# Heads stage of a two-layer encoder trunk: transposes one product group later, first maxima in the last tiles, key tables in ten parts, rotary squares from the latents

## What is computed

```
p = h @ w_in_a                       # h = rmsnorm(x); q_lat 384, kv_lat 256, k_pe 32, ...
q = rmsnorm((rmsnorm(q_lat) @ w_uq).reshape(S, 12, 96)); rope on the last 32 of each head
kv = (rmsnorm(kv_lat) @ w_ukv).reshape(S, 12, 64 + 64)    # k_nope, v
k = rmsnorm(concat(k_nope, k_pe of all heads))            # its mean takes in sum(k_pe ** 2)
k = k * gain, rope on the last 32
o = softmax(q @ k.T * 96 ** -0.5) @ v
```

## Time and profile before

| | |
|---|---|
| median of 3 runs | 3332.96 us (3332.16 to 3334.99) |
| the profiled execution, its span | 3333.53 us, 3331.5 us |
| busy: PE, DVE, ACT, POOL | 96%, 60%, 52%, 42% of the span |
| heads on PE, first product to last transposes | 224.74 to 478.82 us |
| attention, first instruction | 487.49 us |
| DMA share from 262 to 454 us | 0.96 |

### The profile page before, as it was taken

How to read it: one execution, slowest core, us unless ns; L and a number is a source line. 1 busy time by engine, 2 the same in 40 slices (tenths; PEclk the granted TensorE clock), 3 DMA queues, 4 the chain that set the end, 5 groups by cost and what they waited for, 6 DMA issues and landing times. The chain is left out here.

```text
span 3331.5 us, 46492 instructions
## 1 busy us (share of the span) xinstructions
PE 3198.4 (96%) x17548; PEld 2753.4 (83%) x17548; DVE 1991.6 (60%) x2820; ACT 1717.4 (52%) x2514; POOL 1407.4 (42%) x916
## 2 busy tenths in 40 slices
PE   7979979999999999999979999999999979999999
PEld 7978867777777777777769999887888869999787
DVE  5637878888888888888853334445333344333432
ACT  4536646777777777777754455113223234544200
POOL 2227867999999999999920000000111000000000
PEclk9989989999999999999989999999999989999999
DMA  8958983333213333321043223987232243223565
GB/s 305 341 209 294 357 290 80 78 73 77 64 42 66 70 66 68 70 50 42 19 153 101 101 92 108 269 247 227 107 111 98 85 179 126 89 96 105 159 198 152
DMA packets 380334, 454.87 MB, mean 137 GB/s; under 512 B 51800, under 2 KB 317400, under 8 KB 367824
## 3 DMA queue, kind: packets, MB, share of 16 engines
q1 hardware_dynamic: 380112, 451.91, 44.1%
HBM read 262.07 MB, written 189.64 MB: 136 GB/s over the span
## 5 line engine op out<-in xcount | busy, mean ns | idle before, releaser
L1330 POOL TENSOR_TENSOR at_acc<-at_acc,at_ph 128x1024 f32<-128x1024 f32 x288 | 691.2, 2400 | 63.5 <-ACT at_ph L1254 48.1
L1375 DVE TENSOR_TENSOR at_pl<-at_sc,at_ph 128x1024 fp32r<-128x1024 f32 x408 | 498.9, 1223 | 127.0 <-ACT at_sc L1255 122.7
L1254 ACT ACTIVATE at_ph<-at_sc 128x1024 fp32r<-128x1024 f32 x408 | 418.9, 1027 | 289.3 <-PE at_sc L1174 280.9
L1363 DVE TENSOR_REDUCE at_mx<-at_mxp 128x1 f32<-128x512 f32 x816 | 521.5, 680 | 34.4 <-PE at_mxp L1185 34.2
L1255 ACT ACTIVATE at_sc<-at_sc 128x1024 f32<-128x1024 f32 x408 | 415.7, 1019 | 0.0
L1199 PE MATMUL at_o_hi<-at_ph,at_v 128*128 128x512 f32 x816 | 322.9, 396 | 0.6 <-issue 0.6
L1201 PE MATMUL at_o_lo<-at_pl,at_v 128*97 128x512 f32 x816 | 322.2, 395 | 0.0
L1758 POOL TENSOR_TENSOR gm_rstd<-gm_mean,all_mhalf 128x4 f32<-128x4 f32 x40 | 40.3, 1007 | 616.3 <-DVE gm_mean L1898 616.3
L171 PE MATMUL ou_acc<-ou_o_hi,ou_og 128*128 128x512 f32 x640 | 251.7, 393 | 13.4 <-DVE ou_og L2133 12.1
L172 PE MATMUL ou_acc<-ou_o_lo,ou_og 128*128 128x512 f32 x640 | 250.7, 392 | 0.0
L173 PE MATMUL ou_acc<-ou_o_hi,ou_og 128*128 128x512 f32 x640 | 250.5, 391 | 0.0
(11 more groups left out here) (294 smaller groups left out, 8701.7 us busy)
## 6 DMA issues: line engine op xcount, KB each, us to landing
hT<-lat_n_h SPq DMA_DIRECT2D x28, 1024.0 KB, 7.3
h_first<-hT SPq DMA_DIRECT2D x24, 1024.0 KB, 7.8
h_second<-hT SPq DMA_DIRECT2D x24, 1024.0 KB, 7.1
qT<-hd_stq SPq DMA_DIRECT2D x60, 384.0 KB, 6.4
kT<-hd_stk SPq DMA_DIRECT2D x60, 384.0 KB, 6.0
ka_q<-qT SPq DMA_DIRECT2D x120, 192.0 KB, 3.0
sgT<-gm_sg SPq DMA_DIRECT2D x80, 256.0 KB, 2.2
h_first<-omix SPq DMA_DIRECT2D x40, 512.0 KB, 6.2
```

What stands on the lines that cost most here:

```text
L1254: act.activation(ph[:, g], sc[g % 2][:], ACT.Exp, scale=SCALE).then_inc(p_hi, 1)
L1330: pool.tensor_tensor(acc[:, c.slot, :], f32(ph[:, (g - 1) % 4]).rearrange("p b n -> p (b n)") if t == 1 else acc[:, c.slot, :], now, ALU.a ...
L1363: dve.tensor_reduce(mx[:, c.slot, n:n + 1], mxp[n % 2][:], AX.X, ALU.max).then_inc(mx_in, 1)
L1375: dve.tensor_tensor(pl[:, g], sc[g % 2][:], f32(ph[:, g]), ALU.subtract).then_inc(p_lo, 1)
```

## The change

1. On PE each group of transposes stands one product group later: the first two groups of keys after the second and third query group, the third after the first key-value group, the first two groups of queries after the second and third key-value group, the third after the first query group of the next tile. DVE's and ACT's order stays, except at tile 0, where the low values go ahead of the key mean.
2. The first chunk's 16 maxima are made in `heads`, in the banks `pq`, beside the transposes from tile 19's second key-value group on (`BESIDE`), in the order of the key blocks; keys of tiles 12 to 15 are loaded in step 19, and the row of the negated maxima is the last thing that SP issues in the stage. Waiting for the stores, and loading the keys of tiles 16 to 19, go to the start of attention; there chunk 0's first scores stand ahead of the six maxima of chunk 1.
3. The key tables are made two tiles at a time, in ten parts of six instructions: part 0 before the first query root, part p between the query rotation and the key root of tile 2p-2.
4. The mean of the rotary squares is taken by ACT in `latents`, one squaring of 32 columns with a sum per tile, and completed by one DVE instruction.

```diff
+def wait_stored(self, sp):
+    for u in range(2):
+        sp.wait_ge(self.v_out[u], 16 * TILES // 2)
+    for c in range(3):
+        sp.wait_ge(self.q_st[c], 16 * TILES)
+        sp.wait_ge(self.k_st[c], 16 * TILES)
+def row(self, sp, n, slot, quad):
+    sp.wait_ge(self.neg_in, n + 1)
+    for b in range(4):
+        sp.dma_start(f32(self.q[QK:QK + 1, quad, 0, b * P:(b + 1) * P]),
+                     f32(self.neg[:, slot, b:b + 1]), allow_slow_non_contiguous=True
+                     ).then_inc(self.row_in[slot], 16)
...
+    after(act, kpe_in, i)
+    act.activation(junk[:, QL + KVL:], a[:, 1, KVL:KW], ACT.Square, scale=float(QK) ** -0.5,
+                   accum_out=ahead.kpms[:, i:i + 1])
     act.copy(kpe_all[:, i, :], a[:, 1, KVL:KW]).then_inc(kpe_in, 1)
...
+    MAXIMA = sorted(range(16), key=lambda n: n % 4)
+    BESIDE = {(TILES - 1, "q", 0): 2, (TILES - 1, "q", 1): 2, (TILES - 1, "q", 2): 2, (TILES, "k", 0): 2,
+              (TILES, "k", 1): 2, (TILES, "k", 2): 2, (TILES, "q", 0): 1, (TILES, "q", 1): 1, (TILES, "q", 2): 2}
...
-        if t.n in (8, 12, 16):
-            sp.wait_ge(k_st[0], 16 * (t.n - 4))
-            keys.load_first(sp, kT, t.n - 8, t.n - 4)
+        if t.n in (8, 12, 16, 19):
+            last = (t.n + 1) // 4 * 4 - 4
+            sp.wait_ge(k_st[0], 16 * last)
+            keys.load_first(sp, kT, last - 4, last)
     run_tiles(DRAIN, step)
-    for u in range(2):
-        sp.wait_ge(v_out[u], 16 * TILES // 2)
-    for c in range(G):
-        sp.wait_ge(q_st[c], 16 * TILES)
-        sp.wait_ge(k_st[c], 16 * TILES)
-    keys.load_first(sp, kT, 12, TILES)
+    keys.row(sp, 0, 0, 0)
...
-    def queries(t, k_behind):
+    def maximum(n, of, c):
+        for at, piece in maxima_beside(n, of, c):
+            if at == 0:
+                pe.wait_ge(q_out, TILES)
+                pe.wait_ge(q_sq, TILES)
+                pe.wait_ge(keys.q_load[0], 32)
+            pe.wait_ge(keys.kh_load[0], 16 * (piece % 4 + 1))
+            after(pe, keys.mx_in, at - 2)
+            pe.matmul(pq[:, at % G, :], keys.q[0:QK, 0, 0, piece // 4 * P:(piece // 4 + 1) * P],
+                      keys.k0[0:QK, 0, piece % 4 * BLK:(piece % 4 + 1) * BLK], start=True, stop=True
+                      ).then_inc(keys.mx_mm, 1)
+    def queries(t, q_behind, k_behind):
         if t.within(TILES):
             pe.wait_ge(lat_in[t.slot], t.half * 16 + 16)
             after(pe, q_out, t.n)
...
                 if c == G - 1:
                     m.then_inc(q_mm, 1)
-            if k_behind.within(TILES):
-                turn_k(k_behind, c)
-    def keys_values(t, q_behind):
+            if c == 0 and q_behind.within(TILES):
+                turn_q(q_behind, G - 1)
+            if c > 0 and k_behind.within(TILES):
+                turn_k(k_behind, c - 1)
+            maximum(*((t.n - 1, "q", G - 1) if c == 0 else (t.n, "k", c - 1)))
+    def keys_values(t, k_behind, q_behind):
         if t.within(TILES):
             after(pe, k_out, t.n)
             after(pe, v_lo, t.n)
...
                 if c == G - 1:
                     m.then_inc(kv_mm, 1)
-            if q_behind.within(TILES):
-                turn_q(q_behind, c)
+            if c == 0 and k_behind.within(TILES):
+                turn_k(k_behind, G - 1)
+            if c > 0 and q_behind.within(TILES):
+                turn_q(q_behind, c - 1)
+            maximum(*((t.n, "k", G - 1) if c == 0 else (t.n, "q", c - 1)))
     def step(j, u):
-        queries(Tile(j, u), Tile(j, u, -2))
-        keys_values(Tile(j, u), Tile(j, u, -1))
+        queries(Tile(j, u), Tile(j, u, -2), Tile(j, u, -2))
+        keys_values(Tile(j, u), Tile(j, u, -2), Tile(j, u, -1))
...
-    def key_tables():
...
+    def key_tables(part):
+        ts, base = slice(part * PART, (part + 1) * PART), TABLES + part * PART_TABLES
+        cos, sin, rope, pe_rows = cosq[:, ts], sinq[:, ts], krope[:, ts], kpe_all[:, ts]
+        gains_of = lambda n: graw[:, n:n + 1, 0:RP].broadcast_to([P, PART, RP])
+        pool.wait_ge(made, base)
+        pool.tensor_tensor(cos, cos, gains_of(2), ALU.mult).then_inc(made, 1)
+        pool.tensor_tensor(sin, sin, gains_of(3), ALU.mult).then_inc(made, 1)
+        pool.wait_ge(made, base + 2)
+        pool.tensor_tensor(rope, pe_rows, cos, ALU.mult).then_inc(made, 1)
+        pool.wait_ge(made, base + 3)
+        pool.tensor_tensor(cos[:, :, 0:H], pe_rows[:, :, H:RP], sin[:, :, 0:H],
                            ALU.mult).then_inc(made, 1)
-        pool.tensor_tensor(cosq[:, :, H:RP], kpe_all[:, :, 0:H], sinq[:, :, H:RP],
+        pool.tensor_tensor(cos[:, :, H:RP], pe_rows[:, :, 0:H], sin[:, :, H:RP],
                            ALU.mult).then_inc(made, 1)
-        pool.wait_ge(made, 7)
-        pool.tensor_tensor(krope[:], krope[:], cosq[:], ALU.add).then_inc(made, 1)
-        pool.tensor_tensor(sinq[:], kpe_all[:], kpe_all[:], ALU.mult).then_inc(made, 1)
+        pool.wait_ge(made, base + 5)
+        pool.tensor_tensor(rope, rope, cos, ALU.add).then_inc(made, 1)
...
+        pool.wait_ge(made, TABLES + (t.n // PART + 1) * PART_TABLES)
...
         t = Tile(j, u)
+        if t.n == 0:
+            key_tables(0)
         query_root(t)
         query_rope(t)
-        if t.n == 0:
-            key_tables()
+        if t.n % 2 == 0 and t.n // 2 + 1 < PARTS:
+            key_tables(t.n // 2 + 1)
         key_root(t)
         key_rope(t)
     run_tiles(0, step)
+    pool.wait_ge(k_rope, TILES)
+    pool.memset(f32(keys.k0[QK:QK + 1, 0, :]), 1.0).then_inc(keys.ones_in, 1)
...
+    dve.tensor_scalar(kpms[:], kpms[:], EPS, 1.0, ALU.add, ALU.mult).then_inc(squares, 1)
+    dve.wait_ge(squares, 1)
...
+    def maxima(n, of, c):
+        for at, piece in maxima_beside(n, of, c):
+            dve.wait_ge(keys.mx_mm, at + 1)
+            dve.tensor_reduce(keys.mx[:, 0, piece:piece + 1], pq[:, at % G, :], AX.X, ALU.max
+                              ).then_inc(keys.mx_in, 1)
...
-    def key_squares():
-        dve.wait_ge(made, K_TABLES)
...
         if t1.within(TILES):
-            if t1.known and t1.n == 0:
-                key_squares()
+            if t1.n == 0:
+                value_lo(t1)
             key_mean(t1)
         if t2.within(TILES):
             low_k(t2, 0)
-        if t1.within(TILES):
+        maxima(t.n, "k", 0)
+        if t1.within(TILES) and t1.n > 0:
             value_lo(t1)
         if t2.within(TILES):
             low_k(t2, 1)
+            maxima(t.n, "k", 1)
             low_k(t2, 2)
+            maxima(t.n, "k", 2)
         if t.within(TILES):
             query_mean(t)
         if t1.within(TILES):
             low_q(t1, 0)
             key_scale(t1)
+            maxima(t.n, "q", 0)
             low_q(t1, 1)
+            maxima(t.n, "q", 1)
             low_q(t1, 2)
         if t.within(TILES):
             query_scale(t)
+        maxima(t.n, "q", 2)
     run_tiles(DRAIN, step)
+    dve.wait_ge(keys.mx_in, 16)
+    dve.tensor_reduce(keys.neg[:, 0, :], keys.mx[:, 0, :].rearrange("p (q n) -> p q n", q=4), AX.X, ALU.max,
+                      negate=True).then_inc(keys.neg_in, 1)
...
     c0 = Chunk(0)
+    keys.wait_stored(sp)
     load_v(0)
-    row(c0)
     load_q(c0.ahead(2))
+    keys.load_first(sp, kT, 16, TILES)
     load_k(1)
     load_v(1)
...
+            if c.part == 0 or c.n == Chunk.PARTS - 1:
                 pe.wait_ge(kl_load[c.kv], keys_loaded(c))
...
+            if not has_before(c):
+                pe.wait_ge(const_in, 5)
             pe.wait_ge(v_load[c.kv], loaded(c))
...
     c0 = Chunk(0)
-    maximum(c0, range(c0.pieces))
+    pe.wait_ge(keys.ones_in, 1)
+    scores(c0, 0)
     maximum(c0.ahead(1), range(Chunk.LEAD - 16))
-    pe.wait_ge(const_in, 6)
-    scores(c0, 0)
```

More of the change, by code:

```diff
@@ L332, in __init__ @@
         self.kl_load = [s.sem(f"kl_load{u}") for u in range(2)]
+        self.mx = s.sb("mx", [P, 2, 16])
+        self.neg = s.sb("neg", [P, 2, 4], F32R)
+        self.ones_in, self.mx_mm, self.mx_in, self.neg_in = (s.sem(n) for n in ("ones", "mx_mm", "mx_in", "neg_in"))
+        self.row_in = [s.sem(f"row{u}") for u in range(2)]
+        self.v_out = [s.sem(f"v_out{u}") for u in range(2)]
+        self.q_st = [s.sem(f"q_st{c}") for c in range(3)]
+        self.k_st = [s.sem(f"k_st{c}") for c in range(3)]
+    def wait_stored(self, sp):
[10 more added lines that the diff above has]
+                         ).then_inc(self.row_in[slot], 16)
     def load_q(self, sp, qT, head, part, quad):
@@ L582, in heads @@
         gcol = s.sb("gcol", [QK, 1])
-        kpms = s.sb("kpms", [P, TILES])
+        kpms = ahead.kpms
         sqq = s.sb("sqq", [P, QW])
@@ L599, in heads @@
         pt = [s.ps(f"pt{u}", [P, HPG, P]) for u in range(2)]
-        tabs, made, gains, q_mm, kv_mm, q_sq, k_sq, q_red, k_red, q_mean, k_mean, q_rstd, k_rstd = (
-            s.sem(n) for n in ("tabs", "made", "gains", "q_mm", "kv_mm", "q_sq", "k_sq", "q_red", "k_red",
```

(29 more changed lines are left out.)

39 lines of the change are left out of this document (13 added, 26 removed).

## The result

The changed kernel took 3345.35 us in the median of 6 runs (3342.70 to 3350.05), the kernel before 3332.93 us on the same chip (6 runs). The ratio is 1.0039 with a 95% interval from 1.0028 to 1.0049: 12.4 us slower, where +12.7 was predicted. The profiled span is 3341.7 us (3331.5 before).

A forecast was written before the change was run, and what follows sets the result against it. It took PE, DVE and POOL to run at one pace in heads, with no slack. Its terms, -15.0 + 33.7 + 1.8 - 7.8 = +12.7 us, added to the median 3332.96, gave 3345.7 us, range 3322 to 3357.

The forecast's parts named there:

- the one on the transposes: Heads stage: moved transposes lengthen DVE's chain to the low values; a tile takes 13.29 us in place of 11.31.
- The signs named beforehand: Changed profile: q(2) near 247 us, tiles 13.3 us, PE idle about 1.6 us before kv, negated row near 510, scores near 515.
- A: Start of heads: kv(1) follows q(1) at once, so q(2) starts at 246.8 instead of 261.78: -15.0 us.
- B: Steady stretch of heads, 17 tiles from q(2) to q(19), each longer by 1.98 us: +33.7 us.
- C: Key tables on POOL: nine parts of 2.0 us on every second tile, some 0.2 us each: +1.8 us.
- D: End of heads to attention's third scores: 51.1 us after q(19), where today it is 58.95: -7.8 us.
- the waits stay hidden: Heads tiles: low values still reach PE in time, tile 11.3 to 11.9 us, 3310 to 3320 us; chance 0.14.
- half of them: Heads tiles of 12.3 to 13.0 us, the chain 0.3 to 1 us shorter, 3327 to 3339 us; chance 0.15.
- rival 3: POOL in heads: table parts of 2.6 us or more, those tiles 14 us or more, 3352 to 3360 us; chance 0.12.
- rival 4: Start of heads: a stall stays because rotation, tables and first root share POOL; -5 instead of -15, 3355 us; chance 0.04.
- The rule of the Trainium skill: DVE's key scaling waits up to 1.7 us behind each POOL root, low queries 0.25 later: +4.3, 3350 us; chance 0.02.
- The rows: Profile before: POOL's query root stretches from 2267 to 3572 ns while DVE's key scaling stays 939 to 951 ns, so DVE is not held.

The follow-up runs named there:

- Transposes back: The changed kernel with each group of transposes again at the end of its own product group, ten table parts kept: 3322.70 us, 0.9962 against the kernel before.
- the shift alone: The kernel before with only the transposes moved one product group later, tables, squares and maxima as they were: 3367.44 us, 1.0099 against the kernel before.
- low values first: The changed kernel with DVE's low values ahead of the key mean in all tiles instead of tile 0 alone: 3328.24 us, 0.9982 against the kernel before.
- tables at once: The changed kernel with the key tables made for all tiles together after tile 0's query rotation: 3350.81 us, 1.0053 against the kernel before.
- gains first: The changed kernel, transposes at their old place, key tables unsplit, two of six table products moved ahead around the first query root: 3312.90 us, 0.9937.
- transposes back and tables at once: The changed kernel with transposes at the end of their own product group and key tables made for all tiles together: 3313.74 us, 0.9943.

## Why the prediction was right, point by point

**The chain.** The step that decided was the one on the transposes: a tile is as long as the chain from the third query transposes through DVE to the low values. It said 7.63 us from q to kv and 5.66 from kv to q. Measured: 7.60 in tile 19 (474.25 to 481.85) and 5.61 (13.21 - 7.60). The tile of the chain alone is 13.21, 13.29 was predicted. Transposes back and the shift alone show that the shift makes the tile longer, the latter without any other part of the change; low values first shows which part of DVE's work lies in the chain. The signs named beforehand are there: q(2) at 247.04, the negated row at 510.72, the first scores at 515.66. What misled in the profile before was the earlier trace rows: PE 191.98 of 192 busy, on top of a chain exactly as long.

**The terms of the sum,** as differences between the starts on PE:

| term | predicted | measured |
|---|---|---|
| heads begins, q(0) | 0 | +1.2 (225.97, 224.74) |
| A, q(2) | -15.0 | -14.7, the start above included |
| B, seventeen tiles | +33.7 | +32.3 (17 x 1.90) |
| C, table parts | +1.8 | +2.7 (14.39 - 13.21 = 1.2 in the third tile, all of it counted here, then 8 x 0.19) |
| D, q(19) to the third scores | -7.8 | -7.25 |
| third scores | +12.7 | +12.98 |

A was right to 0.3 us only because two small errors cancel: the stage began 1.2 later, and q(2) came 1.0 us earlier after q(0) than I had it (q(2) - q(0): 21.07, predicted 22.06). B and C together are 17 x 2.06 = +35.0, predicted +35.5. The part was sized at 2.0 us and measured 1.90, and its way into the tile (every second round of POOL just longer than PE's) is the one seen, through the query root. D is 0.6 us off in a stretch of 51, and a sum of two: the maxima in the drain save 9.0 us (50.23 for 59.26, transposes back in both), and the shift takes some 3 back (51.70 for 48.56, ten parts in both).

**What was not seen.** The parts' price depends on the shift. With it the tile has slack on POOL and nine parts cost under 3 us; with the transposes back they cost 1.4 us each, and 8 us more than the tables at once by the medians, 5.1 in the traces from q(0) to q(19) (228.05 and 222.94). So the four parts of the change do not add up: the shift costs 24.5 us by itself beside ten parts (-12.1 to +12.4), 37 beside tables at once (-20.1 to +17.0), 32.6 on the kernel before. The prediction priced the parts only in the company in which they stood, which was enough for its number, but says nothing of the version without the shift.

**The rivals.** That the waits stay hidden, or half of them, is refuted by 30.5 us of waits; rival 3 (POOL binds) by a part of 1.90 us, not 2.6 or more, and a root that pushes DVE by only 0.2 us; rival 4 has a trace of truth in the 2.73 us wait of the third tile. The rule of the Trainium skill (SBUF — State Buffer, the section "SBUF: two separate sides"), by which the engine that issues first keeps the port and the other is blocked for the whole instruction, comes out in two ways. For products the traces agree with it from both sides. Where a POOL product begins inside DVE's scaling it stands until that ends, 0.25 us become 1.36. Where one begins just ahead of DVE's scaling, DVE stands, 1.35 us become 2.71 (gains first). But where DVE's key scaling falls into a running query root (355.23 into 354.73 to 358.30) it takes its usual 0.94 to 0.95 and the root grows from 2.27 to 3.57 us: for the root the rule does not hold, and why it differs from a product stays open. It is not the length alone, for the 1.57 us product did hold DVE. The rows were right to be followed for the root, which is what the prediction asked of them; that DVE is never held would have been too much.

## What to carry to other kernels

A bank that comes free 0.14 us before it is needed is a second bound of the same size, and an engine at 100% hides it; before an instruction is moved, the chain through its consumers has to be added up, on both halves of the loop, from the starts of one tile. What fills the idle time of an engine costs nothing only if it neither is held by the engine that is waited for nor holds that one. And of a change in several parts each should be timed alone and with each partner: here the maxima in the drain (9 to 12 us) and the squares (8 us) were worth having, and the shift of the transposes (24 to 37 us) cost more than both brought.

## What was not expected of the hardware

In some executions the granted clock falls to half for some 3 us in the latents, after PE has waited about 2 us for DVE. The window from 88 to 90 us in the changed kernel, and behind it in the run with the transposes back and tables at once, columns as in the earlier trace rows:

```profile
88.00:90.00 2.00, 2.00 (x10) 2.00 (x9) 2.00 (x3) 0.58 (x1) 0.00 (x0) 0.50 0.80 322
```

```profile
88.00:90.00 2.00, 2.00 (x16) 2.00 (x15) 2.00 (x3) 0.59 (x1) 0.00 (x0) 1.00 0.75 313
```

The same code stands before the same wait (2.02 us in both) and runs on at half clock (1.2 GHz) in one and at full clock in the other: 10 matmuls in 2 us against 16. Six of the nine profiled kernels with squares in the latents show such a fall, after this wait or after one of 1.9 to 2.7 us that ends near 47 us, and none of the three without. The times do not bear out that the squares cost anything (3313.74 with, 3313.78 without), and what decides it stays open. The fall is the larger part of the +1.2 in the first line of the table: from the end of that wait to the end of PE's last wait for DVE in the latents it takes 131.82 us in the changed kernel and 130.25 in the other. It is not all, for the run with tables at once shows no such fall and begins heads at 225.82.
